# A decoder block on one core: the steps of the chunked delta rule with a signal per result, quarter products and masks in other places

## The reference, cut to what matters

```python
diff = gc[..., :, None] - gc[..., None, :]
decay = jnp.where(incl, jnp.exp(jnp.where(incl, diff, 0.0)), 0.0)
kb = k * beta[..., None]
A = jnp.where(strict, jnp.einsum('bhnid,bhnjd->bhnij', kb, k) * decay, 0.0)
T = lax.linalg.triangular_solve(A + eye, ...)          # (I + A)^-1
u = T @ (v * beta);  w = T @ (kb * exp(gc))
qk = (q @ k^T) * decay;  q_dec = q * exp(gc);  k_dec = k * exp(gc[-1] - gc)
def step(S, inp):
    v_new = u_n - w_n @ S
    o_n = qd_n @ S + qk_n @ v_new
    S = S * gt_n + k_dec^T @ v_new
```

## Time and profile before

| | |
|---|---|
| median of three runs | 721.01 us (719.75 to 723.03) |
| the profiled execution | 722.8 us, span 720.7 us |
| PE busy (matmul) | 622.4 us, 86% |
| DVE, ACT, POOL busy | 318.5, 244.1, 44.6 us |
| mean granted PE clock | 0.943 |
| moved by DMA | 155.9 MB |

### The profile page before, as it was taken

How to read it: one execution, slowest core, us unless ns; L and a number is a source line. 1 busy time by engine, 2 the same in 40 slices (tenths; PEclk the granted TensorE clock), 3 DMA queues, 4 the chain that set the end, 5 groups by cost and what they waited for, 6 DMA issues and landing times.

```text
span 720.7 us, 13819 instructions
## 1 busy us (share of the span) xinstructions
PE 622.4 (86%) x5639; PEld 511.6 (71%) x5639; DVE 318.5 (44%) x717; ACT 244.1 (34%) x565; POOL 44.6 (6%) x92
## 2 busy tenths in 40 slices
PE   2899999899999988999799999997887947759575
PEld 2899999798988978888688989875454514325141
DVE  4534349899869757451533465115221111011112
ACT  5335548476775443313213282014010100001002
POOL 8200000000000001110202010000000000000000
PEclk9799999899999999999999999998999979788896
DMA  9855453133343331101115138897799999999981
GB/s 288 253 168 162 149 168 117 59 118 119 104 130 114 123 117 60 60 3 59 58 61 176 59 114 276 328 421 301 276 423 420 421 421 422 422 422 422 421 360 58
DMA packets 69691, 155.94 MB, mean 216 GB/s; under 512 B 7171, under 2 KB 56437, under 8 KB 57349
## 3 DMA queue, kind: packets, MB, share of 16 engines
q1 hardware_dynamic: 65792, 154.36, 57.2%
q10 hardware_dynamic: 3844, 0.82, 0.6%
HBM read 154.12 MB, written 1.05 MB: 215 GB/s over the span
## 4 chain that ended last, share of the span: by engine, by line
PE 64%; DMA 19%; DVE 7%; ACT 5%; issue 3%; POOL 1%; SPq 0%; DVEq 0%; POOLq 0%; ACTq 0%
PE bank L758 29%; DMA arena<-in_expert_w_down_dram 18%; PE bank L1118 6%; PE bank L928 4%; PE bank L747 4%; PE bank L740 4%; PE bank L1099 2%; PE bank L870 2%; PE bank L847 2%; PE bank L906 1%; PE bank L1084 1%; PE bank L1125 1%; DVE w_lo L287 1%; PE bank L815 1%; DMA arena<-in_meta_tokens_dram 1%
## 5 line engine op out<-in xcount | busy, mean ns | idle before, releaser
L758 PE MATMUL bank<-uT_hi,w_hi 128*128 128x272 f32 (+1 forms) x576 | 176.8, 307 | 6.8 <-issue 5.2
L758 PE MATMUL bank<-uT_lo,w_hi 128*128 128x272 f32 (+1 forms) x576 | 166.6, 289 | 0.0
L758 PE MATMUL bank<-uT_hi,w_lo 128*128 128x272 f32 (+1 forms) x576 | 166.3, 289 | 0.0
L287 DVE TENSOR_TENSOR w_lo<-arena,w_hi 128x1024 fp32r<-128x1024 f32 x80 | 98.8, 1236 | 47.8 <-ACT w_hi L282 47.4
L758 PEld LDWEIGHTS bank<-uT_hi,w_hi 128*128 128x128 f32 x576 | 111.0, 193 | 10.2 <-issue 7.9
L758 PEld LDWEIGHTS bank<-uT_lo,w_hi 128*128 128x128 f32 x576 | 111.2, 193 | 1.6 <-issue 0.5
L758 PEld LDWEIGHTS bank<-uT_hi,w_lo 128*128 128x128 f32 x576 | 111.2, 193 | 0.0
L282 ACT ACTIVATE w_hi<-arena 128x1024 fp32r<-128x1024 f32 x80 | 83.8, 1051 | 4.5 <-PE bank L758 4.2
L1118 PE MATMUL bank<-arena 128*32 128x512 f32 x256 | 41.8, 813 | 37.5 <-DMA arena<-in_expert_w_down_dram 36.5
L1099 PE MATMUL bank<-arena 128*32 128x256 f32 x1024 | 56.9, 380 | 0.0
L1118 PEld LDWEIGHTS bank<-arena 128*32 128x32 f32 x256 | 10.5, 143 | 62.8 <-issue 61.4
(11 more groups left out here) (318 smaller groups left out, 863.3 us busy)
## 6 DMA issues: line engine op xcount, KB each, us to landing
arena<-in_w_in_dram SPq DMA_DIRECT2D x36, 1024.0 KB, 5.3
arena<-in_expert_w_gate_dram SPq DMA_DIRECT2D x32, 1024.0 KB, 24.3
arena<-in_expert_w_up_dram SPq DMA_DIRECT2D x32, 1024.0 KB, 24.1
arena<-in_expert_w_down_dram SPq DMA_DIRECT2D x32, 1024.0 KB, 21.4
arena<-in_w_branch_attn_dram SPq DMA_DIRECT2D x4, 1024.0 KB, 5.0
arena<-in_w_branch_dn_dram SPq DMA_DIRECT2D x4, 1024.0 KB, 6.4
arena<-in_w_out_dram SPq DMA_DIRECT2D x4, 1024.0 KB, 5.0
arena<-in_x_dram SPq DMA_DIRECT2D x4, 512.0 KB, 5.1
```

What stands on the lines that cost most here:

```text
L287: nc.vector.tensor_tensor(w_lo[q % NSPLIT], src, w_hi[q % NSPLIT].bitcast(F32), ALU.subtract).then_inc(w_lo_ready, 1)
L758: last = pe.matmul(ps[:, 0:b.shape[2]], a[:, c, :], b[:, c, :], start=(c == 0 and i == 0), stop=(c == NC - 1 and i == 2))
```

## The change

Steps and order. x1 joins s7, and w exists for the meta tokens alone. The steps of chunk 1's s0 move ahead of chunk 0's q. Filler halves follow a group: three behind s0 (two for the meta tokens), two behind t2, one behind each other group; three halves are left behind the last.

```diff
-        STEPS = ["s0", "s1", ..., "s7", "x1", "t1", "x2", "t2", "x3", "t3", "w", "v", "o", "q"]
+        STEPS = ["s0", "s1", ..., "s7", "t1", "x2", "t2", "x3", "t3", "v", "o", "q"]
+        GROUPS = [[("meta", 0, s)] for s in META_STEPS]
+        for s in STEPS[:-1]:
+            GROUPS.append([(0, 0, s), (0, 1, s)])
+        GROUPS += [[(1, 0, "s0"), (1, 1, "s0")], [(0, 0, "q"), (0, 1, "q")]]
+        for s in STEPS[1:]:
+            GROUPS.append([(1, 0, s), (1, 1, s)])
+        SIGNALS = {
+            "dve": {"s0": ("masked", "a0"), "s1": ("a",), "s2": ("a16",), "s3": ("a2", "p"), ...
+            "act": {"s0": ("decay", "grow"), "s2": ("at",), ..., "s7": ("x1", "tt"), ..., "o": ("sq", "kept"), "q": ("root",)},
+            "pool": {"s2": ("q_scaled",), "s5": ("off",), "q": ("gated",)},
+        }
-            while given < 2 * len(filler) and given * (len(groups) - 4) < i * 2 * len(filler):
-                MIX_ORDER.append(("half", (filler[given // 2], given % 2)))
-                given += 1
-            MIX_ORDER += [("dn", k) for k in group]
+        BEHIND_GROUP = {"s0": 3, "t2": 2}
+            MIX_ORDER += [("dn", k) for k in group]
+            if i < H:
+                MIX_ORDER.append(("spread", N_DN + i))
+            count = BEHIND_GROUP.get(group[0][2], 1) - (1 if group[0] == ("meta", 0, "s0") else 0)
+            MIX_ORDER += halves[:count]
+            del halves[:count]
```

```diff
-                for engine in ("act", "dve", "pool"):
-                    wait_step(pe, engine, (t, c, s), before=True)
+                need = lambda engine, *names: [wait_dn(pe, engine, t, c, name) for name in names]
                 elif s == "s1":
-                        last = pe.transpose(X[:, h, :], w[1][:, h, :], ident)
-                    if t != "meta":
-                        last = each(Z, kT, qT)
+                    need("dve", "a0")
+                        for q in range(2):
+                            last = pe.matmul(Zs[rows, h, :], w[1][rows, h, rows], ident_c[rows, :], ..., tile_position=(q * Q, q * Q))
                 elif s == "s2":
-                        last = pe.transpose(Y[:, h, :], w[2][:, h, :], ident)
+                    need("dve", "a")
+                    last = both(Ys, small(c, 2, 0), ident_c.unsqueeze(1).broadcast_to([P, 4, Q]))
+                    if t != "meta":
+                        need("act", "grow")
+                        last = each(X, kT, qT)
                 elif s == "s7":
+                    need("dve", "t16")
+                    last = both(Xs, T, ident_c...)
+                    if t != "meta":
+                        need("pool", "off")
+                        last = both(Zs, small(c, 4, 0), T)
...
+                    if t != TT - 1:
+                            last = pe.transpose(Y[:, h, :], kT(h), ident)
+                elif s == "x2":
+                    need("dve", "t32")
+                    both(Zs, small(c, 4, 1), T)
+                    last = each(Y, kT, lambda h: S[:, 4 * c + h, :])
                 elif s == "w":
-                    else:
-                        last = each(X, buf(2), buf(0))
                 elif s == "v":
-                        pe.matmul(Z[:, h, :], w[0][:, h, :], w[4][:, h, :], start=True, stop=False)
-                        last = pe.matmul(Z[:, h, :], w[6][:, h, :], S[:, 4 * c + h, :], start=False, stop=True)
+                    need("dve", "t128")
+                    last = each(Z, buf(0), buf(2))
                 elif s == "o":
+                    need("act", "v")
+                    need("pool", "q_scaled")
```

```diff
                 if s == "s0":
-                    link(tt(b(1), Y, b(0), ALU.mult))
-                    last = tt(b(1), b(1), each_head(strict), ALU.mult)
+                    mark(tt(b(1), Y, each_head(strict), ALU.mult))
+                    wait_dn(dve, "act", t, c, "decay")
+                    follow()
+                    done(tt(b(1), b(1), b(0), ALU.mult))
                 elif s == "s1":
-                    last = tt(b(2), X, per_head(nbeta), ALU.mult)
-                    if t != "meta":
-                        last = tt(b(3), Z, b(0), ALU.mult)
+                    done(tt(piece(2, 0), Zs, per_head(nbeta, Q), ALU.mult))
+                elif s == "x2":
+                    for h in range(n):
+                        last = stt(w[2][:, h, :], Y[:, h, :], nbegc[:, k0 + h:k0 + h + 1], dv_tok[:, t, 4 * c + h, :], ALU.mult, ALU.add)
                 elif s == "t3":
-                    last = tt(b(4), dv_tok[:, t, hs, :], per_head(beta), ALU.mult)
```

ACT takes the four exponentials first and exp(X) behind them, copies diagonal quarters in s2 at once, copies the output in o ("kept") beside its squares, and scales v by beta when it evicts v's transposes (two copies of 128x128 in place of one of 128x256). The "ln and exp" table is still preloaded at the first chain's q. POOL waits for named results:

```diff
+                if s == "s2":
+                    wait_dn(pool, "pe", t, c, "s2")
+                    wait_dn(pool, "act", t, c, "grow")
+                    pool.tensor_tensor(q, q, w[7], ALU.mult).then_inc(dn_pool[c], 1)
+                elif s == "s5":
+                    pool.tensor_tensor(small(c, 4, 0), small(c, 6, 1), off32_c..., ALU.mult)
+                    pool.tensor_tensor(small(c, 4, 1), small(c, 6, 1), off64_c..., ALU.mult).then_inc(dn_pool[c], 1)
```

More of the change, by code:

```diff
@@ L124, in hybrid_block @@
         gc2 = new(2, NCOL)
-        egc, begc, kdec, egt, ngc, nbeta = (new(NCOL) for _ in range(6))
+        egc, nbegc, kdec, egt, ngc, nbeta = (new(NCOL) for _ in range(6))
         ba_meta = new(16)
@@ new lines, in hybrid_block, with signals, count_of @@
+        NOT_META, NOT_CHUNK, NOT_LAST = ("p", "grow", "x1", "q_scaled", "off"), ("bv",), ("kd", "state")
+        def signals(engine, t, step):
+            if engine == "pe":
+                return [step]
+            skip = NOT_META if t == "meta" else NOT_CHUNK + (NOT_LAST if t == TT - 1 else ())
+            return [name for name in SIGNALS[engine].get(step, ()) if name not in skip]
+        def count_of(engine, t, c, name):
+            made = [(chunk, name_) for chunk, chain, step in DN if chain == c for name_ in signals(engine, chunk, step)]
+            return made.index((t, name)) + 1
@@ L378, in diagonal @@
             return a[q * Q:(q + 1) * Q, :, q * Q:(q + 1) * Q]
[L380 to L401, removed]
         every, first_half, rest = slice(None), slice(0, H // 2), slice(H // 2, H)
@@ L412, in hybrid_block @@
         MIX_ORDER = []
[L413 to L417, removed]
-            while given < 2 * len(filler) and given * (len(groups) - 4) < i * 2 * len(filler):
-                MIX_ORDER.append(("half", (filler[given // 2], given % 2)))
-                given += 1
+        BEHIND_GROUP = {"s0": 3, "t2": 2}
+        halves = [("half", (n, half)) for n in filler for half in range(2)]
+        for i, group in enumerate(GROUPS):
             MIX_ORDER += [("dn", k) for k in group]
@@ L423, in hybrid_block @@
                 MIX_ORDER.append(("spread", N_DN + i))
-        MIX_ORDER += [("half", (filler[k // 2], k % 2)) for k in range(given, 2 * len(filler))]
+            count = BEHIND_GROUP.get(group[0][2], 1) - (1 if group[0] == ("meta", 0, "s0") else 0)
+            MIX_ORDER += halves[:count]
+            del halves[:count]
+        MIX_ORDER += halves
         BEHIND = []
@@ L1259, in tr_out @@
                 elif kind == "dv":
-                    last = act.activation(dv_tok[:, :, i, :], ps[:, 1:3, :], ACT.Copy)
+                    if i == 0:
+                        act.wait_ge(g_ready, 1)
+                    for t in range(TT):
+                        k = t * H + i
+                        last = act.activation(dv_tok[:, t, i, :], ps[:, 1 + t, :], ACT.Copy, scale=beta[:, k:k + 1])
                 else:
@@ L1348, in dn @@
             def dn(t, c, s):
[L1349 to L1350 removed]
                 w = work[c]
                 X, Y, Z = (bank[2 + 3 * c + i][:, :].rearrange("p (h i) -> p h i", h=4) for i in range(3))
+                Xs, Ys, Zs = (bank[2 + 3 * c + i][:, 0:4 * Q].rearrange("p (h i) -> p h i", h=4) for i in range(3))
                 n = 1 if t == "meta" else 4
[L1354 to L1357 removed]
+                done = lambda ins: ins.then_inc(dn_act[c], 1)
                 if s == "s0":
[L1361 to L1363 removed]
+                    wait_dn(act, "dve", t, c, "masked")
                     for h in range(n):
@@ L1387, in dn @@
+                    done(act.activation(w[6], Y, ACT.Square))
+                    done(act.activation(w[3], Y, ACT.Copy))
                 elif s == "q":
-                    link(act.activation(w[7][:, 0:n, :], Z[:, 0:n, :], ACT.Ln, scale=1.0 / P, bias=c_eps))
-                    last = act.activation(w[7][:, 0:n, :], w[7][:, 0:n, :], ACT.Exp, scale=-0.5)
-                last.then_inc(dn_act[c], 1)
+                    if c == 0:
+                        act.preload_act_table_set("natural_log_exp_and_others")
@@ L1393, in _ @@
+                    wait_dn(act, "pe", t, c, s)
+                    link(act.activation(w[5], Z, ACT.Ln, scale=1.0 / P, bias=c_eps))
+                    done(act.activation(w[5], w[5], ACT.Exp, scale=-0.5))
             act.wait_ge(qk_ready, N_DN)
```

275 lines of the change are left out of this document (156 added, 119 removed).

## The result

The changed kernel takes 711.48 us (median of 4, 709.59 to 712.34), the kernel before beside it 722.02 us (4 runs, 719.75 to 724.12): ratio 0.9857, 95% interval 0.9824 to 0.9891, clear of no change. The forecast of 710.4 against 721.0 is a ratio of 0.9853. The profiled execution took 712.34 us against 722.8 before, 10.5 less.

What follows compares the result with a forecast made beforehand. PE bounds the mixed stretch, losing time to single waits; the experts' weight stream follows its end. Terms -2.1 - 14.5 + 6.3 + 0.3 - 0.6 = -10.6 us take 721.0 to 710.4 us, range 704 to 716 (the forecast's own 707 to 714).

Steps and rivals of the forecast that it cites:

- The rival that the stream of weights keeps its own time: Experts' weight stream bound by the wall clock, not released buffers, so the mixed stretch's gain is lost: 721.0 us, chance 0.05.
- the slower one by the granted clock: More and smaller bursts of quarters lower PE's granted clock; with ten low stretches 727.4 us, chance 0.04.
- The waits that go, -14.5: PE's waits from 236 to 455 us, in s1, for POOL, for gating and a late tile, all go: -14.5 us.
- What is late next, +6.3: New PE waits: +1.1 at meta step m, +1.9 before tile 66 behind chunk 0's q, +3.3 before tile 76.
- The rival in which every wait goes: The three new waits are smaller than reckoned and the clock stays up: -18.0, 703.0 us, chance 0.13.
- PE's own work, -2.1: PE's products and transposes in both chunks -3.6, five more bursts of quarters +1.0, meta step +0.5: -2.1 us.
- v's copies, +0.3: Eight copies of v become sixteen half as wide, scaled by beta: 0 to +0.8, taken as +0.3 us.
- The clock, -0.6: The clock drop at 386 to 391 us, behind a POOL wait that goes, may vanish: 0 to -1.7, taken as -0.6.
- The tail's loads: Tile 73's Tanh between chunk 1's roots: two table loads between the roots, one before the last Tanh, 1.28 us each.
- the rival of longer table changes: Each of the tail's three table loads is followed by as long a pause again: +3.8, 714.2 us, chance 0.07.
- One half tile covers a step: In steps s2 to t3 a half tile (1.42 to 1.93 us) covers ACT copies of 0.38 and DVE sums of 0.42.
- the rival (715.4): DVE slows beside POOL, so one half tile no longer covers a step; five of eight pieces reach PE: +5, chance 0.15.

## Why the prediction was right, point by point

- **What bounds, and that the end follows.** Right. The stretch lost 12.2 us, the rest stayed at 291. The rival that the stream of weights keeps its own time is out, and so is the slower one by the granted clock: there is one low stretch between 236 and 420 us, as before, in spite of more bursts.
- **The waits that go, -14.5.** Right to the row. By parts, each from one pair of profiled executions, the filler behind s0 was worth 5.4 in the old kernel, POOL's earlier mask 3.2, s2's named signal 1.1; s0's own order 1.3 in the new one. Naming the signals, the edit in front of the description, is worth least: 1.1 for s2's in the old order, 0.8 for all of them in the new. Chunk 0's gating (1.2) and the late tile (1.6) were not taken apart.
- **What is late next, +6.3.** Measured 1.1, 1.8 and 2.9 against 1.1, 1.9 and 3.3: 5.8, each at its place and by its maker, and each removed by one move at 1.0, 1.85 and 2.03 us (which left 0.7 of the third). The rival in which every wait goes falls with these rows: queues in order were exact about who stood behind whom.
- **PE's own work, -2.1.** The direction is right, the size is short. From the stretch: -12.18 + 14.5 - 5.8 = -3.5 are left for it, and PE's busy time says the same, 182.19 - 178.72 = 3.47 less. By an estimate some 1.1 of that belongs to the waits. The records of PE's products overlap while it runs on, and the last one before a wait lasts to its modelled end: in the earlier trace rows eight pieces started at 267.72 and end at 268.78, from which the 2.38 are counted, but at the earlier trace rows's 1.78 for 16 pieces they would have been through at 268.6, 2.56 before the next one. That is about 0.16 a wait that counts as work, and seven waits fewer. It leaves some -2.4 beside the forecast -2.1. Bursts at 0.20 held (0.21 by the run). The Trainium skill's rule in "TensorEngine Tiling (Array Packing)", "Key Properties", that a change of tiling mode drains the engine, agrees in its direction: a change of mode less is time less. The transposes and the rearrangement of w and v were not undone by themselves.
- **v's copies, +0.3.** The term that was mis-sized: the narrow scaled copy is hardly shorter than the wide one, 0.372 against 0.382 us in the mean, so a "narrower copy" was no reason for the low end. In the changed kernel's timeline the pair takes 0.64, and PE waits for such a pair before it transposes v's next tile:

```profile
206.15 0.64 ACT L1300 ACTIVATE arena<-bank,arena 128x128 f32<-128x128 f32 x2
```

  The place where PE waits:

```profile
217.14 0.41 PE L770 MATMUL bank<-arena 128*128 128x128 f32 x2 [1.75 <-ACT arena L1300]
```

  In the kernel before the same place waited for DVE, and less:

```profile
215.50 0.44 PE L773 MATMUL bank<-arena 128*128 128x128 f32 x2 [1.28 <-DVE arena L1636]
```

  Against 0.38 for one of the earlier trace rows a pair costs +0.26. The wait grew by 0.47, and one behind ACT before L844 from 0.18 to 0.33: +0.6 together, as much as the kernel lost between its first tile and the meta s0 (0.63), within the bounds of 0 to 0.8 but at their upper part. The total alone would not show it, since that way took 212.5 to 213.1 us in the kernels with the old copies and 212.4 to 213.3 in those with the new.
- **The clock, -0.6.** 0 in the profiled executions. The drop didn't go, there was one behind the new wait of 2.9 us at the same price of 1.7. My "equal wait" reasoning looked only at the wait that went, not at those that came.
- **The tail's loads.** Three in PE's way, none with a pause: the rival of longer table changes, with the Trainium skill's 2.66 us for a change ("ScalarE: Activation LUTs", "What ACT_TABLE_LOAD costs"), is out at 1.29. The order of the loads was not the forecast one.
- **One half tile covers a step.** Right, and the rival (715.4) is out: no wait inside s2 to t3. The conflict is there: in chunk 0's s2 of the changed kernel DVE's L1810 took 1.41 us beside POOL's scaling of q, where the same operation took 0.42 in front of it.

```profile
274.14 0.42 DVE L1810 TENSOR_TENSOR arena<-arena 128x256 f32<-128x256 f32 x1
276.35 1.41 DVE L1810 TENSOR_TENSOR arena<-arena 128x256 f32<-128x256 f32 x1
```

  No PE wait comes of it. POOL's eight masks took 0.72 to 0.85 us each, and PE waited for none.
- **The sum.** -2.1 - 14.5 + 6.3 + 0.3 - 0.6 = -10.6 was forecast; measured -3.5 - 14.5 + 5.8 + 0.6 + 0 = -11.6 from the change, and +1.0 of the late first tile and 0.2 at the end, which are not its own. So the change itself brought 1.0 more than forecast, and the 1.2 us that are not its own hid that: that the total came within 0.1 us (10.5 against 10.6) is in part luck, and the spread of the runs is wider than that.

## What to carry to other kernels

Write out every engine's queue around a change in the order of work: the waits that a new order makes can be priced from it as well as those that it removes, and here each was then removed, but for 0.7 us of the last, by moving one entry or a few of a list (702.1 us instead of 711.5, the joined bursts included). What an exact wait is worth depends on who is late; place the filler behind the longest chain and the side engine's work a group earlier first, and name signals after that. Prices of single waits don't add up where one wait covers the next (6.8 us came of 9.7), and they do where each has an origin of its own (6.6 came of 6.0).

## What the runs showed of the hardware

- **The clock's drop comes and goes with the same wait.** Behind the tail's 2.9 us the clock was 0.63 for 4.6 us in the changed kernel and 1.00 with the bursts joined, with evictions 64 and 65 moved, or with the split moved. In the run that waits for everything it fell at 405.4, inside that same wait, and cost 3.1 us. In the kernel before there was one drop of 1.7 us; without only 1.9 or only 3.3 us of its waits there was none, and with the filler moved there was one at 278 us. These are single executions of each kernel, and executions of one kernel differ too: the kernel before had mean granted clocks from 0.941 (725.2 us) to 0.957 (719.1 us). Whether the edit or the execution decides is open; no run was made for it. So a profiled pair can differ by 1.7 us that the edit doesn't explain by a wait.
- **Of POOL and DVE the one that starts second is the slow one.** In the kernel before, POOL's mask took 0.74 with DVE at work on data in banks beside it and 1.61 when it started behind a low half of a split on DVE, which kept its 1.23 us:

```profile
298.51 0.74 POOL L679 TENSOR_TENSOR arena<-arena 128x256 f32<-128x256 f32 x1 [22.26 <-DVE arena L1782]
299.72 1.23 DVE L287 TENSOR_TENSOR w_lo<-arena,w_hi 128x1024 fp32r<-128x1024 f32 x1
299.91 1.61 POOL L679 TENSOR_TENSOR arena<-arena 128x256 f32<-128x256 f32 x1 [0.66 <-DVE arena L1782]
```

  In the changed kernel POOL's scaling of q started first, at 276.04, and took 1.43; DVE's L1810 started at 276.35 and took 1.41 for 0.42, as shown above.
  In the run that waits for everything I expected 1.4 us before s6 from the mean of such rows (1.15); L674's masks took 0.73 there and PE didn't wait for them. The mean of two kinds of rows was no duration of either.
- **A root whose Ln has no preload costs two loads**, 1.28 us before the Ln and 1.28 before its Exp.
